# Early expert rows dealt to other places of VectorE's list, and dense-stage expert rows handled two blocks later

## What is computed

```python
def peer_ffn(xn, wq, subkeys, u, v):          # per block of 128 tokens
    q = (tb @ wq).reshape(128, 8, 2, 128)
    sc = einsum('thpd,pnd->thpn', q, subkeys)
    sv, si = top_k(sc, 16)                    # per half key
    cand = sv[:, :, 0, :, None] + sv[:, :, 1, None, :]
    cv, ci = top_k(cand, 16)                  # per head
    e = i1 * 128 + i2;  g = softmax(cv)       # 128 experts per token
    h = einsum('thkd,td->thk', u[e], tb)
    a = gelu(h) * g
    return einsum('thk,thkd->td', a, v[e])
```

## Time and profile before

| | |
|---|---|
| median of 3 runs | 3882.74 us (3880.98 to 3892.97) |
| the profiled execution's own time | 3891.12 us |
| its span | 3889.4 us |
| mean granted TensorE clock | 0.93 |
| TensorE matmuls / weight loads busy | 3322.5 us (85%) / 2257.1 us (58%) |
| VectorE busy | 2688.9 us (69%) |
| GpSimd busy | 1544.3 us (40%) |
| ScalarE busy | 975.0 us (25%) |
| DMA moved | 1199.22 MB, mean 308 GB/s |

### The profile page before, as it was taken

The page is one execution under the profiler, slowest core; times in us unless marked ns, Lnnn a source line. Parts: engine busy times, 40 slices in busy tenths (PEclk is TensorE's granted clock), DMA queues, the critical chain, the costliest instruction groups (busy, mean ns, idle before and its releaser), DMA issues. The chain is left out here.

```text
span 3889.4 us, 45277 instructions
## 1 busy us (share of the span) xinstructions
PE 3322.5 (85%) x15374; PEld 2257.1 (58%) x15398; DVE 2688.9 (69%) x4868; ACT 975.0 (25%) x1832; POOL 1544.3 (40%) x1202
## 2 busy tenths in 40 slices
PE   8898998986888877665757289999999999999998
PEld 7445888974565565544456255555555555555554
DVE  0453878754488566453636888888888888888886
ACT  1452112124122324523655111111111111111112
POOL 0000277720322577578772233333333333333331
PEclk9899999988999988877878699999999999999999
DMA  7897499957888678767586799999999999999996
GB/s 257 339 415 293 168 379 386 384 194 244 333 300 291 184 217 239 171 205 141 140 199 174 248 384 385 381 390 387 388 391 390 392 389 382 390 387 378 384 393 240
DMA packets 488231, 1199.22 MB, mean 308 GB/s; under 512 B 199400, under 2 KB 263320, under 8 KB 425752
## 3 DMA queue, kind: packets, MB, share of 16 engines
q0 software_dynamic: 166768, 674.44, 47.3%
q1 hardware_dynamic: 187760, 502.17, 34.6%
q10 hardware_dynamic: 133568, 20.84, 3.4%
HBM read 1126.54 MB, written 71.83 MB: 308 GB/s over the span
## 5 line engine op out<-in xcount | busy, mean ns | idle before, releaser
L2405 DVE SCALAR_TENSOR_TENSOR d_both<-d_both,k_xn 128x1024 f32<-128x1024 f32 x384 | 460.4, 1222 | 253.4 <-DMA d_both<-peer_uv,d_idx 253.3
L2553 PE MATMUL d_ps<-d_x_high,d_u_high 128*128 128x512 f32 x1024 | 452.4, 442 | 67.4 <-ACT d_u_high L2507 67.4
L2384 POOL DMA_INDIRECT d_both<-peer_uv,d_idx x384 | 451.8, 1176 | 140.2 <-issue 113.1
L1651 POOL DMA_INDIRECT G<-c_cellg,c_cell x256 | 446.4, 1744 | 145.7 <-issue 73.7
L2389 POOL DMA_INDIRECT d_values<-peer_uv,d_idx x128 | 146.5, 1145 | 896.5 <-DVE k_acc L2426 888.6
L2422 DVE SCALAR_TENSOR_TENSOR d_acc<-d_both,d_aw,d_acc 128x1024 f32<-128x1024 f32 x384 | 470.6, 1281 | 4.6
L2571 PE MATMUL d_ps<-k_ring,k_xd 128*128 128x512 f32 x1024 | 451.0, 593 | 0.0
L2571 PE MATMUL d_ps<-d_v,k_xd 128*128 128x512 f32 x1024 | 450.2, 593 | 0.0
L2553 PE MATMUL d_ps<-d_x_low,d_u_high 128*128 128x512 f32 x1024 | 402.0, 393 | 0.0
L1840 DVE SCALAR_TENSOR_TENSOR k_ring<-k_ring,c_xn 128x1024 f32<-128x1024 f32 x128 | 156.1, 1221 | 285.2 <-DMA k_ring<-peer_uv,c_row 284.9
L2571 PEld LDWEIGHTS d_ps<-d_v,k_xd 128*128 128x128 f32 x1024 | 194.7, 190 | 221.8 <-issue 216.9
(11 more groups left out here) (402 smaller groups left out, 5723.6 us busy)
## 6 DMA issues: line engine op xcount, KB each, us to landing
c_chunk<-wq SPq DMA_DIRECT2D x128, 512.0 KB, 6.4
k_ring<-u_blocks SPq DMA_DIRECT2D x128, 512.0 KB, 7.7
s_kc<-sb_kT SPq DMA_DIRECT2D x32, 1024.0 KB, 10.1
s_vc<-sb_v SPq DMA_DIRECT2D x32, 1024.0 KB, 8.3
c_chunk<-w_m SPq DMA_DIRECT2D x64, 512.0 KB, 5.4
k_ring<-v_blocks SPq DMA_DIRECT2D x64, 512.0 KB, 8.6
d_gb<-G SPq DMA_DIRECT2D x64, 512.0 KB, 8.0
d_v<-v_blocks SPq DMA_DIRECT2D x64, 512.0 KB, 9.0
```

Source lines behind the costliest of these rows:

```text
L1651: pool.indirect_dma_start(out=grid, out_offset=bass.IndirectOffsetOnAxis(ap=cell[q][:, s:s + 1], axis=0), in_=cell_g[q][:, s:s + 1], in_of ...
L2384: pool.indirect_dma_start(out=both[par][T][:], out_offset=None, in_=a["peer_uv"], in_offset=bass.IndirectOffsetOnAxis(ap=idx_body[half][:, ...
L2405: last = nc.vector.scalar_tensor_tensor(both[x % 2][T][:, 0:D], both[x % 2][T][:, 0:D], 1.0, xn[:, T], ALU.mult, ALU.mult, accum_out=h[:, ...
L2553: last = nc.tensor.matmul(ps[:, HB + x % 2, :], u_high[:, k], x_part[:, k], start=(k == 0 and n == 0), stop=False)
```

## The change

**Early rows.** Their products are dealt by another table: for an iteration six numbers, of products ahead of the two gates, between the two gates, at each of the six hooks, ahead of the weights, behind them, and ahead of the residual addition. None stands in the search. Up to row 37 (CALM = 38) six slots of the ring serve, then three. GpSimd's list becomes: 20 rows, 40 scatters, 6 times (4 rows, 1 scatter), 20 scatters, 31 times (row, scatter), 25 scatters, 31 times (row, scatter), 25 scatters, 22 times (row, scatter), and the 56 scatters that are left. The first one-hots, which lie in slots that early rows now use, wait for product 38, on VectorE and on ScalarE.

**Dense stage.** In turn b the rows' products, their gelu and their additions are those of block b - 2 (BEHIND = 2); gate, low part and takes stay. Behind the loop stand two turns of rows alone. Buffers, gathers and their order are unchanged.

```diff
-    BETWEEN, DOTS, DOTS_BESIDE = 29, {4: 16, 5: 20, 6: 19, 7: 21, 8: 10}, {5: 1, 6: 2, 7: 2, 8: 2}
+    DOTS = {4: (0, 2, 0, 3, 3, 6), 5: (0, 2, 0, 10, 5, 7), 6: (3, 3, 2, 5, 2, 6), 7: (3, 3, 2, 5, 2, 6), 8: (5, 4, 2, 7, 0, 0)}
+    CALM = 38
+    early_slot = lambda k: k % 6 if k < CALM else 3 + (k - CALM) % 3
...
-    EB, EARLY_AT = 3, 3
...
                 def early_rows(n):
-                    for k in range(asked[0], min(asked[0] + n, P)):
-                        if k >= EB:
-                            pool.wait_ge(dotted, k - EB + 1)
+                    for k in range(asked[0], asked[0] + n):
+                        s = early_slots[k]
+                        if s in early_slots[:k]:
+                            pool.wait_ge(dotted, k - early_slots[:k][::-1].index(s))
...
-                early_rows(DOTS[4] + EB)
+                early_rows(20)
...
-                        if s % rows_after[0] in rows_after[1]:
-                            early_rows(1)
-                for h in range(8):
-                    scatter_head(0, h, (5, (0, 2, 4)))
-                for h in range(8):
-                    scatter_head(1, h, (4, (1,)))
-                early_rows(P)
+                scatters(40)
+                for n in range(6):
+                    early_rows(4)
+                    scatters(1)
+                scatters(20)
+                for n in range(31):
+                    early_rows(1)
+                    scatters(1)
+                scatters(25)
+                for n in range(31):
+                    early_rows(1)
+                    scatters(1)
+                scatters(25)
+                for n in range(22):
+                    early_rows(1)
+                    scatters(1)
+                scatters(2 * P - sent_on[0])
...
                         if c >= DEEP:
                             dve.wait_ge(spread_done, c - DEEP + 1)
+                        else:
+                            dve.wait_ge(dotted, CALM)
...
-                        due = DOTS.get(i, 0)
-                        dots(due * passed[0] // BETWEEN - due * (passed[0] - 1) // BETWEEN)
...
-                    gated(i)
+                    dealt = DOTS.get(i, (0,) * 6)
+                    dots(dealt[0])
+                    gated(i, lambda: dots(dealt[1]))
...
-                        dots(DOTS_BESIDE.get(i, 0))
+                        dots(dealt[2])
                     experts_of(i - 2, beside_products)
+                    dots(dealt[3])
                     weigh(i - 2)
+                    dots(dealt[4])
...
                         logs(t + 1, 0)
+                        dots(dealt[5])
                         residual(i)
```

and in `dense`, with `add_rows`, `products` and ScalarE's list indexed to match:

```diff
+    BEHIND = 2
...
-                        if number(k) and x == 0:
-                            low(b, j)
-                            products(k, x)
-                        else:
+                        opening = number(k) and x < BEHIND
+                        if not opening:
+                            products(k, x - BEHIND)
+                        if not (number(k) and x == 0):
                             y = (x - 1) % BODY
-                            products(k, x)
                             gate(b - 1, y // GB, y % GB, k if x else k - 1)
-                            low(b, j)
+                        low(b, j)
...
-                        add_rows(k, x)
+                        if not opening:
+                            add_rows(k, x - BEHIND)
...
-                gate(P - 1, 1, GB - 1, NG // 2 - 1)
+                for x in range(BEHIND):
+                    products(P // BODY, x - BEHIND)
+                    if x == 0:
+                        gate(P - 1, 1, GB - 1, NG // 2 - 1)
+                    add_rows(P // BODY, x - BEHIND)
...
-                        act.wait_ge(prod_done, b + 1)
-                        nc.scalar.activation(ge[:, x], h[:, x], ACT.Gelu).then_inc(row_gelu, 1)
+                        if not (number(k) and x < BEHIND):
+                            rows_gelu(b - BEHIND, (x - BEHIND) % BODY)
```

More of the change, by code:

```diff
@@ L1341, in decide @@
     among = lambda j: AMONG.get(j, 0)
-    BETWEEN, DOTS, DOTS_BESIDE = 29, {4: 16, 5: 20, 6: 19, 7: 21, 8: 10}, {5: 1, 6: 2, 7: 2, 8: 2}
+    DOTS = {4: (0, 2, 0, 3, 3, 6), 5: (0, 2, 0, 10, 5, 7), 6: (3, 3, 2, 5, 2, 6), 7: (3, 3, 2, 5, 2, 6), 8: (5, 4, 2, 7, 0, 0)}
+    CALM = 38
+    early_slot = lambda k: k % 6 if k < CALM else 3 + (k - CALM) % 3
+    early_slots = [early_slot(k) for k in range(P)]
+    early_uses = lambda k: len(range(early_slots[k], REST, RB)) + early_slots[:k + 1].count(early_slots[k])
     NB = 5
     RB = 6
-    EB, EARLY_AT = 3, 3
     QUAD, DEEP, TS = 4, 3, 32
@@ L1639, in _ @@
+                    asked[0] += n
                 pool.wait_ge(rows_ready, 1)
                 pool.wait_ge(summed, REST)
-                early_rows(DOTS[4] + EB)
[L1643 to L1647, removed]
-                    else:
-                        pool.wait_ge(scattered[q], 256 * h)
-                    for s in range(16 * h, 16 * h + 16):
+                early_rows(20)
@@ L1651, in scatter_head, with scatters @@
+                sent_on = [0]
+                def scatters(n):
+                    for at in range(sent_on[0], sent_on[0] + n):
+                        q, s = at // P, at % P
+                        if s == 0:
+                            pool.wait_ge(dve_r.sem, dve_r.at(SENT[q], "index"))
+                            pool.wait_ge(dve_g.sem, dve_g.at(SENT[q], "g"))
+                        elif s % 16 == 0:
+                            pool.wait_ge(scattered[q], 16 * s)
                         pool.indirect_dma_start(out=grid, out_offset=bass.IndirectOffsetOnAxis(ap=cell[q][:, s:s + 1], axis=0),
@@ L1683, in step, with gated @@
                         dve.wait_ge(dve_r.sem, dve_r.at(i, name))
-                def gated(i):
+                def gated(i, beside=lambda: None):
                     dve.wait_ge(gate_in, 16 * i)
@@ L1688, in gated @@
                     merged(nc.vector.tensor_tensor(gate[:, 1], wide(6), gate[:, 1], ALU.mult))
+                    beside()
                     dve.wait_ge(eaten, MERGE_AT[i] + 8)
@@ L1837, in dots @@
                     for k in range(dots_done[0], dots_done[0] + n):
-                        s = EARLY_AT + k % EB
-                        dve.wait_ge(filled[s], 16 * (len(range(s, REST, RB)) + k // EB + 1))
+                        s = early_slots[k]
+                        dve.wait_ge(filled[s], 16 * early_uses(k))
                         nc.vector.scalar_tensor_tensor(ring[:, s], ring[:, s], 1.0, xn0[:], ALU.mult, ALU.mult, accum_out=h0[:, k:k + 1]).then_inc(dotted, 1)
@@ L2401, in products @@
                 def products(k, x):
+                    use, x = 4 * k + x // 2, x % BODY
                     for T in range(LOADED):
-                        dve.wait_ge(filled[x % 2][T], 16 * (4 * k + x // 2 + 1))
+                        dve.wait_ge(filled[x % 2][T], 16 * (use + 1))
                         last = nc.vector.scalar_tensor_tensor(both[x % 2][T][:, 0:D], both[x % 2][T][:, 0:D], 1.0, xn[:, T], ALU.mult, ALU.mult,
@@ L2409, in add_rows @@
                 def add_rows(k, x):
[L2411 to L2416, removed]
+                    r, use, x = BODY * k + x, 4 * k + (x + 1) // 2, x % BODY
+                    first = number(r) and r == 0
+                    dve.wait_ge(row_gelu, r + 1)
+                    nc.vector.tensor_tensor(aw[:, x, :, None], ge[:, x, :, None], gw[:, 1:, bass.ds(r, 1)], ALU.mult).then_inc(weighed, 1)
+                    dve.wait_ge(weighed, r + 1)
+                    if first:
                         dve.wait_ge(acc_in, 16 * FETCHED)
@@ L2419, in add_rows @@
                     for T in range(LOADED):
-                        if not (first and k == 0):
-                            dve.wait_ge(added[1 - x % 2][T], 4 * k + (x + 1) // 2)
+                        if not first:
+                            dve.wait_ge(added[1 - x % 2][T], use)
                         nc.vector.scalar_tensor_tensor(acc[T + 1][:], both[x % 2][T][:, D:], aw[:, x, T:T + 1], acc[T + 1][:], ALU.mult, ALU.add).then_inc(added[x % 2][T], 1)
[L2423 to L2426, removed]
+                    dve.wait_ge(filled0, 16 * (r + 1))
+                    if not first:
+                        dve.wait_ge(added0, r)
+                    nc.vector.scalar_tensor_tensor(acc[0][:], values0[:], h0[:, bass.ds(r, 1)], acc[0][:], ALU.mult, ALU.add).then_inc(added0, 1)
                 def low(b, j):
@@ L2532, in _ @@
                     body(k)
+                for x in range(BEHIND):
+                    rows_gelu(P - BEHIND + x, BODY - BEHIND + x)
                 for T in range(FETCHED):
```

12 lines of the change are left out of this document (8 added, 4 removed).

## The result

The changed kernel takes 3904.18 us (median of 8 runs, 3896.32 to 3915.33); the kernel before, beside it, 3883.96 (8 runs, 3875.59 to 3892.97). The ratio is 1.0046, interval 1.0027 to 1.0065: **slower by some 18 us (10 to 25)**, where 3877 was forecast and 3902 was the upper end. The profiled execution took 3904.96 us, with a span of 3903.3.

What follows compares the result with a forecast made beforehand. It took GpSimd's queue order to make early rows late in routing, and DMA and TensorE to be nearly full in the dense stage. Part 1's -6 us plus part 2's 0, from 3882.7, gave 3877; 8-in-10 range 3844 to 3902.

Steps and rivals of the forecast that it cites:

- The three pieces: Routing stage: GpSimd stands 49, 79 and 50 us before rows 41, 72 and 103, waiting for products 38, 69 and 100.
- y(5): Routing stage: the residual after which iteration 6 can run, forecast at 1415 where it was 1433.7.
- 12 earlier or 1 earlier; I take the middle, 6: Routing stage's end, set by GpSimd: 12 or 1 us earlier depending on the scatter's price; 6 us earlier was taken.
- GpSimd becomes the end: Rival, 15%: GpSimd's 56 scatters behind row 127, dearer heads, held searches and no burst gain make it 26 us later: 3903.
- the own case: The prediction's main forecast, 60%, with its own range 3861 to 3893; 38 of the 60 within 11.6 us of no change.
- The rows are in time: Rival, 9%: in the routing stage GpSimd does not stand 178 us, so row waits go; a third gained, 59 us: 3818.
- The waits only change their place: Rival, 4%: the waits only move elsewhere, giving 3883 us.
- The standstill of 16 us: Dense stage's end: TensorE does two chunks, then stands 16 us for a take behind the four final scalings.
- the end 42.0 us behind the last addition: Dense stage: the kernel ends 42.0 us after the last row addition, where it was 41.7.
- at first 7 us, and 4 once the third turn's gather binds: Dense stage's start: the row stream is delayed 7 us at first, then an estimated 4.
- Less 4.5, as the last two turns have two low parts and two takes fewer: Dense stage's end: lighter last two turns save 4.5 us, offsetting the 4 us delay of the row additions.
- the lag decouples TensorE: Rival, 12%: gathers land sooner, so half to all of 46.7 us of low-part waits goes: 3830 to 3854, say 3845.

Runs made afterwards that it cites:

- rows_fewer16: First part alone (early rows, dense stage as before), with the last sixteen scatters of the second tile left out: 3884.56 us, ratio 0.9999 against the kernel before.
- lag_only: Kernel before with only the dense-stage rows put two blocks behind, routing stage as before: 3893.34 us, ratio 1.0008.
- lag_tail: Dense-stage rows two blocks behind, routing stage as before, the last group's four takes moved ahead of the final scalings: 3873.19 us, ratio 0.9961 against the kernel before.
- no_gates_loaded: Kernel before without the dense stage's loads of gates G from the third group on: 3908.31 us, ratio 1.0053.
- rows_shift3: First part alone, GpSimd's list moved by three rows so the scatter bursts precede rows 41, 72 and 103: 3782.20 us, ratio 0.9731 against the kernel before.
- every_second: Kernel before with an early row behind every second of the second tile's scatters instead of every fourth: 3803.02 us, ratio 0.9807.

## Why the prediction was wrong

**The queue order and its waits: right.** The three pieces were forecast at 49, 79 and 50 us and measured 51.2, 71.6 and 51.7. The steps hold to 10 us: product 38 ended at 1464.0 by the forecast (1456.2), row 44 at 1517.8 (1511.7), product 69 at 1698.6 (1690.2), row 75 at 1763.2 (1758.4), row 106 at 1983.0 (1974.7), row 127 at 2060.1 (2058.7), y(8) at 2070.7 (2067.8). y(5) came 29 us earlier than before by the clock and some 23 by length of stage, more than the 15 to 20 forecast. Some luck is in these times: y(4) came 11.7 us earlier in its stage (290.3 us after the first residual addition, 302.0 before) where the prediction took 5, an estimate. Without it the sum would have missed by 7 us more. That GpSimd ends the stage: right, and rows_fewer16 shows it.

**The first step that failed is the term "12 earlier or 1 earlier; I take the middle, 6".** It stood for GpSimd's end, and that came not 6 us earlier but 8 to 10 later in its stage (1208.9 and 1211.4, against a mean of 1201.5). The bursts did gain what was reckoned. By the trace of after, the 77 scatters between rows 41 and 44, 72 and 75, 103 and 106 took 1.58 us each on average, where all of them took 1.744 before. But the prediction counted that gain on one side only. A mean stayed at 1.744 for the rest, and the rest was no longer average:
- The 75 scatters between rows 44 and 71, 75 and 102, 106 and 127 lie beside VectorE's products and took 1.95 each: 15 us more than at 1.744, which takes back the 12.5 that the bursts gain. The other 104 took 1.69 each, so the mean over all 256 was 1.735 after: 2 us less in all, where the prediction had 0 to 11. A split mean must be split on both sides.
- The waits for a sixteen became dearer. The heads inside the bursts waited 5.9, 5.6, 5.3, 6.3, 4.5 and 1.6 us, one in the tail 10.3; the sum over all is 58.3 in 14, 4.2 each, for the 3.35 assumed: 11 us more. It holds beyond this profile: the sum is 51.3 to 60.7 us in the five others with bursts, and 41.6 to 45.9 in the eight without. Why a single one takes 1.6 or 10.3 is not shown.
- The last scatter took 7.2 us to land, not 3.4: 4 us more.

By mean prices the sum had GpSimd's end 1 us earlier. With 11 and 4 us more for the waits, 2 less for the scatters and 7 less for y(4), it comes to 5 later; measured are 8 to 10. The few us between are not accounted for, and no run takes these terms apart.

The rival "GpSimd becomes the end" (15%, 3903) had the right place, the dearer heads and bursts without a net gain; its third term, searches held by other engines, did not occur. It was not a rival in mechanism at all, only the same case with prices from the upper ends, and the own case gave them too little: 8 of its 60 for slower. Of the other two, "The rows are in time" (9%) fell with the 174.5 us that GpSimd stood. "The waits only change their place" (4%) was right in what it names, VectorE's 284.9 and 287.3 us, but it had no loss.

**Part 2: the steady turn was right, the sum of the ends was not.** The standstill of 16 us (measured 18.4) and the end 42.0 us behind the last addition (41.0, and 41.5 in lag_only) were right. Of "at first 7 us, and 4 once the third turn's gather binds" the 7 was right and the 4 failed: the last addition of row 0 ended 6.8 us later in its stage, and that of row 48 11.0. "Less 4.5, as the last two turns have two low parts and two takes fewer" failed too: with nothing else for VectorE to do, it waited for the gathers, and the last two turns were 2.6 us shorter together (3.5 in lag_only), not 4.5. Over five profiles with lag 2 the last addition ends 1657.5 to 1667.2 us after the stage's start (mean 1662.3), over six without lag 1653.0 to 1659.9 (mean 1657.0): some 5 us later, where 0 was forecast. The two ranges overlap, and by its times lag_only is +3 us with 0 inside its interval, so this second step is less sure than the first.

**The rival "the lag decouples TensorE"** fell: TensorE's wait for low parts over 2300 to 3800 us is 40.4 before and 43.6 in lag_tail. But the argument against it, the share of 0.98, was a poor one, as no_gates_loaded shows; the argument from the order within a turn was enough.

**The rule of the two sides.** The Trainium skill (SBUF — State Buffer, "SBUF: two separate sides") has, beside the two-port modes, a VectorE instruction with two SBUF inputs contend for the shared port pair with a GpSimd instruction that reads SBUF. The prediction weighed only the narrow form. By the timelines of all 14 profiles, 950 scatters beside an idle VectorE took 1.57 us (1.55 to 1.61), 35 that lay mostly beside a row product, whose two inputs are in SBUF, 1.95, and 13 beside the gate product, one of whose inputs is in PSUM, 1.57. That agrees with the wider form. But the search's MAX8, with one input, goes with 1.67 (133 scatters), so the number of inputs is not the whole of it, and no run changes it alone.

## What to carry to other kernels

In an in-order queue, what matters of a wait is what stands behind it: put work that waits for nothing (the scatters) ahead of the instruction that will wait (row 41), not behind it. Here a shift by three entries turned a loss of 15 us into a gain of 106. And when work is taken off one engine's path, write down what the other engine has left to do at the end: slack of 121 us was gone in the changed kernel, with three standstills of 51 to 72, and in rows_shift3 and every_second too, without them. A price that depends on the neighbour (1.58 or 1.95) must be applied to both kinds of places, or to neither.

## What the runs showed of the hardware

- A DMA share of 0.98 was no bound: with a twentieth of a turn's bytes gone it fell to 0.94 and the turn did not shorten (12.88 and 12.99 us).
- A scatter's issue on GpSimd took 1.56 to 1.57 us on average beside an idle VectorE, in each of the 14 profiles, and 1.95 beside VectorE's row products.
- A wait for sixteen accumulating scatters took 0.5 to 10.3 us in the kernel after, and the last ones of the stage 7.2. The Trainium skill (DMA: Bandwidth & Descriptors, "Anatomy of one DMA — SWDGE (gpsimd) path") puts most of a transfer's fixed cost, some 2 us, down to the receipt of the write, heaviest where the target is HBM. Most waits here are longer than that figure, and no run separates the receipt from the rest.
